# Five query projections moved into the last delta head, and the loads of the next six moved ahead of the attention block

## What is computed

```
p = x @ w_in                         # columns split among all heads
A: gated DeltaNet, 8 heads of 128    # q, k, v, z from p; causal conv; chunked delta rule
B: sparse attention, 16 query heads  # q = p[..., nq], K/V of three branches from p
h = sigmoid(gA) * o_A + sigmoid(gB) * o_B
x = LayerNorm(alpha * x + h @ w_out)
x = LayerNorm(alpha * x + MoE(x))    # 64 experts, top 6
```

## Time and profile before

| | |
|---|---|
| Time, median of 3 (lowest, highest) | 2173.21 us (2172.13, 2180.12) |
| The profiled execution's own time | 2190.67 us |
| Its span | 2188.9 us |
| PE busy | 1900.0 us, 87% |
| DVE, ACT, POOL busy | 798.4, 549.1, 336.3 us |
| Delta heads 0 to 7 | about 148 to 897 us of the span |
| Attention projections (L1391) | 904 to 1024 us of the span |

### The profile page before, as it was taken

One profiled execution on the slowest core, in us unless ns is written; L12 is line 12 of the kernel. 1 busy time (PEld: TensorE's weight loads), 2 busy tenths in 40 slices (PEclk: granted clock), 3 DMA queues, 4 the chain that ended last, 5 costly groups with the idle time before them and its releaser, 6 DMA issues. The chain is left out here.

```text
span 2188.9 us, 27560 instructions
## 1 busy us (share of the span) xinstructions
PE 1900.0 (87%) x10610; PEld 1295.2 (59%) x10610; DVE 798.4 (36%) x1903; ACT 549.1 (25%) x1266; POOL 336.3 (15%) x365
## 2 busy tenths in 40 slices
PE   7599989999898967799998897899998889888978
PEld 4277777777777756588886665546544333434423
DVE  0025444453444541101658874426322222222106
ACT  1121323313223131102656662402011111111110
POOL 0001011010100100100314544400111111111101
PEclk9799999998999975799998998999999999999998
DMA  3531102111021000740530014770699999999946
GB/s 107 161 92 30 50 22 59 52 30 51 22 59 32 1 22 0 169 103 11 161 111 6 1 59 154 250 264 22 282 384 420 417 417 403 407 411 403 402 160 260
DMA packets 160370, 353.95 MB, mean 162 GB/s; under 512 B 36488, under 2 KB 113968, under 8 KB 134320
## 3 DMA queue, kind: packets, MB, share of 16 engines
q1 hardware_dynamic: 140368, 291.88, 36.2%
q0 software_dynamic: 19872, 60.31, 7.7%
HBM read 333.09 MB, written 35.27 MB: 168 GB/s over the span
## 5 line engine op out<-in xcount | busy, mean ns | idle before, releaser
L720 PE MATMUL bank<-xT,arena 128*128 128x272 f32 x1280 | 326.6, 407 | 1.7 <-DMA arena<-in_w_in 1.1
L2488 PE MATMUL bank<-arena,kvt 128*64 128x512 f32 (+1 forms) x816 | 268.6, 630 | 45.0 <-issue 44.1
L720 PEld LDWEIGHTS bank<-xT,arena 128*128 128x128 f32 x1280 | 243.6, 197 | 48.7 <-DMA arena<-in_w_in 1.3
L2488 PEld LDWEIGHTS bank<-arena,kvt 128*64 128x64 f32 (+1 forms) x816 | 91.1, 152 | 185.3 <-issue 185.3
L1055 POOL TENSOR_TENSOR arena<-arena 128x512 f32<-128x512 f32 x48 | 52.4, 1092 | 645.4 <-DVE arena L1157 447.3
L1391 PE MATMUL bank<-xT,arena 128*128 128x272 f32 x512 | 119.6, 397 | 13.5 <-DMA arena<-in_w_in 13.5
L2567 PE MATMUL bank<-arena,kvt 128*64 128x512 f32 (+1 forms) x408 | 128.1, 598 | 2.4 <-issue 2.1
L2884 DVE SCALAR_TENSOR_TENSOR kvt<-kvt,arena,bank 128x256 f32<-128x256 f32 x37 | 17.8, 480 | 282.6 <-ACT kvt L2674 282.6
L1391 PEld LDWEIGHTS bank<-xT,arena 128*128 128x128 f32 x512 | 98.6, 193 | 34.2 <-DMA arena<-in_w_in 13.6
L2488 PE MATMUL bank<-xT,kvt 128*64 128x512 f32 (+1 forms) x208 | 104.5, 661 | 15.9 <-issue 15.9
L2340 POOL DMA_INDIRECT hT<-x_rows,rows_i x37 | 37.6, 1017 | 392.3 <-DVE rows_i L2815 392.3
(11 more groups left out here) (510 smaller groups left out, 3242.0 us busy)
## 6 DMA issues: line engine op xcount, KB each, us to landing
arena<-in_w_exp_gate SPq DMA_DIRECT2D x51, 1024.0 KB, 13.8
arena<-in_w_exp_up SPq DMA_DIRECT2D x51, 1024.0 KB, 27.3
arena<-in_w_exp_down SPq DMA_DIRECT2D x51, 1024.0 KB, 26.3
arena<-in_w_in SPq DMA_DIRECT2D x48, 512.0 KB, 4.1
kvt<-in_w_exp_down SPq DMA_DIRECT2D x13, 1024.0 KB
xT<-in_w_exp_gate SPq DMA_DIRECT2D x13, 1024.0 KB
xT<-in_w_exp_up SPq DMA_DIRECT2D x13, 1024.0 KB
arena<-y_rows SPq DMA_DIRECT2D x6, 1536.0 KB, 15.0
```

The lines of the kernel that those rows point to most:

```text
L720: last = mm(banks[2 * (i % 2) + half][:, 0:HALF], wh[blk % RING][:, k, :], xT[:, k, half * HALF:(half + 1) * HALF], start=(k == 0), stop=( ...
L2488: last = mm(banks[2 + 4 * (t % 2)][cols, :], xgT[:, k, cols], ewgu[i % EBUF][:, :, k], start=(k == 0), stop=(k == KD - 1))
```

## The change

It names five of the eight query blocks (`NQ_BEHIND` = 2, 3, 4, 5, 6) that are now computed behind the delta rule of head 7, with `part(8, j)`. `load_head(8)` loads them, `save_queries` copies them out into `qT` at once (the places of blocks 2 to 6 lie over the conv inputs `raw` of heads 6 and 7, so it waits until these have been read). The remaining three query blocks (0, 1, 7) and the eight merge blocks stay in the attention block, eleven in all (`ATT_BLOCKS`). The first six of the eleven are loaded in the delta block, in SP's stream of head 7, as their slots come free, and SP waits for these loads before it leaves the block. The other five are loaded in the attention block, behind `Wx` and `page_p`, which now come first.

```diff
+NQ_BEHIND, NQ_AHEAD = (2, 3, 4, 5, 6), (0, 1, 7)
+ATT_BLOCKS = len(NQ_AHEAD) + 8
...
+            def await_free(i):
+
+                done_h, m = divmod(i - RING, 5)
+                sp.wait_ge(pr_banked, 6 * done_h + (UNIT[m] if done_h < H else m) + 1)
...
+                    if h == H:
+                        load_query(sp, NQ_BEHIND[n], i, wh_in)
+                        continue
...
-                if h + 2 < H:
+                if h + 2 <= H:
                     load_head(h + 2)
+                if h == H - 1:
+                    for p in range(RING):
+                        await_free(FIRST_ATT + p)
+                        load_attention(sp, p, wh_in)
...
+            for i in range(FIRST_ATT, FIRST_ATT + RING):
+                sp.wait_ge(wh_in[i % RING], landed_by(i))
...
             def part(h, j):
 
-                if h == H:
-                    return
...
+            def save_queries(n):
+
+                i = 6 * H + n
+                if n == 0:
+                    sc.wait_ge(conv_done, H - 1)
+                    sc.wait_ge(cg_ready, H - 1)
+                if n == 2:
+                    sc.wait_ge(conv_done, H)
+                    sc.wait_ge(cg_ready, H)
+                sc.wait_ge(pr_banked, i + 1)
+                for half in range(2):
+                    last = actv(qT[:, NQ_BEHIND[n], half * HALF:(half + 1) * HALF], banks[2 * (i % 2) + half][:, 0:HALF], ACT.Copy)
+                last.then_inc(pr_saved, 1)
...
-            for n in range(16):
-                blk = n
-                pe.wait_ge(wh_in[blk % RING], 16 * sum(KVH if b < G else 1 for b in range(blk % RING, blk + 1, RING)))
+            for n in range(ATT_BLOCKS):
+                blk = FIRST_ATT + n
+                if n >= RING:
+                    pe.wait_ge(wh_in[blk % RING], 16)
```

The new loaders, called from SP's stream:

```diff
+        def load_query(sp, j, i, landed):
+
+            src = w_cols[:, :, COL_NQ:COL_NQ + D].rearrange("p k (g j d) -> j p k g d", g=KVH, j=G)[j]
+            for g in range(KVH):
+                sp.dma_start(wh[i % RING][:, :, g * HD:g * HD + HD], src[:, :, g]).then_inc(landed[i % RING], 16)
+
+        def load_merge(sp, m, i, landed):
+
+            c0 = COL_MG + D + m * P
+            sp.dma_start(wh[i % RING], w_cols[:, :, c0:c0 + P]).then_inc(landed[i % RING], 16)
+
+        def load_attention(sp, p, landed):
+
+            if p < len(NQ_AHEAD):
+                load_query(sp, NQ_AHEAD[p], FIRST_ATT + p, landed)
+            else:
+                load_merge(sp, p - len(NQ_AHEAD), FIRST_ATT + p, landed)
```

More of the change, by code:

```diff
@@ L497, in tok, with landed_by @@
             return (t * P, P if t < 4 else NS_TOK)
+        w_cols = io["w_in"][0].rearrange("(k p) n -> p k n", p=P)
+        def load_query(sp, j, i, landed):
[10 more added lines that the diff above has]
+                load_merge(sp, p - len(NQ_AHEAD), FIRST_ATT + p, landed)
+        FIRST_Q = 5 * H
+        FIRST_ATT = FIRST_Q + len(NQ_BEHIND)
+        def landed_by(i):
+            first_merge = FIRST_ATT + len(NQ_AHEAD)
+            return 16 * sum(2 if FIRST_Q <= b < first_merge else 1 for b in range(i % RING, i + 1, RING))
         def load_gate_up(sp, i, which):
@@ L630, in load_head @@
                     if i >= RING:
-                        done_h, m = divmod(i - RING, 5)
-                        sp.wait_ge(pr_banked, 6 * done_h + UNIT[m] + 1)
+                        await_free(i)
+                    if h == H:
+                        load_query(sp, NQ_BEHIND[n], i, wh_in)
+                        continue
                     sp.dma_start(wh[i % RING], w[:, :, c0 + h * P:c0 + h * P + P]).then_inc(wh_in[i % RING], 16)
+                if h == H:
+                    return
                 if h >= 2:
@@ L707, in part @@
             def part(h, j):
-                if h == H:
-                    return
                 n, quarter = divmod(j, 4)
                 half, k0 = quarter // 2, quarter % 2 * 4
-                i = 6 * h + UNIT[n]
+                i = 6 * h + (UNIT[n] if h < H else n)
                 blk = 5 * h + n
                 if quarter == 0:
-                    pe.wait_ge(wh_in[blk % RING], 16 * (blk // RING + 1))
+                    pe.wait_ge(wh_in[blk % RING], landed_by(blk))
                     if i >= 2:
@@ L909, in _ @@
             actv(convw[:, :], banks[5][:, 0:96], ACT.Copy).then_inc(cw_ready, 1)
+            def save_queries(n):
[10 more added lines that the diff above has]
+                last.then_inc(pr_saved, 1)
             def save(h, unit):
                 if h == H:
+                    if unit != 3:
+                        save_queries(UNIT.index(unit))
                     return
@@ L1310, in _ @@
         def _(sp):
-            w = io["w_in"][0].rearrange("(k p) n -> p k n", p=P)
             sp.dma_start(page_all[:, :], io["page_table"].rearrange("(o b) p -> o (b p)", o=1).to_broadcast([P, NB * NPG])).then_inc(ids_in, 16)
             sp.dma_start(quad_cmp, io["quad_cmp"]).then_inc(ids_in, 16)
-            for n in range(16):
[L1316 to L1333, removed]
+            w1 = io["nsa_cmp_w1"][0].rearrange("s (r j u d) e -> s r (u d) j e", r=2, j=8, u=2)
+            for s in range(2):
+                for r in range(2):
+                    sp.dma_start(Wx[:, s, :, r * HD:(r + 1) * HD], w1[s, r]).then_inc(w1_in, 16)
+            rows = cmp_rows.rearrange("(n a r) c -> a n (r c)", a=4, r=4)
+            for a in range(4):
+                sp.dma_start(page_p[32 * a:32 * a + 32], rows[a]).then_inc(rows_p_in, 16)
+            for p in range(RING, ATT_BLOCKS):
+                sp.wait_ge(prj_banked, p - RING + 1)
+                load_attention(sp, p, wh_in)
+            sp.wait_ge(prj_banked, ATT_BLOCKS)
             sp.dma_start(pos_rows[0:32], io["nsa_cmp_pos"][0].rearrange("s (m u) d -> (s m) (u d)", u=2)).then_inc(c2_in, 16)
@@ L1393, in _ @@
                 last.then_inc(prj_banked, 1)
-            pe.wait_ge(prj_saved, 16)
+            pe.wait_ge(prj_saved, ATT_BLOCKS)
             for br in range(2):
@@ L1674, in _ @@
             step = Steps(sc, act_step)
-            for n in range(16):
+            for n in range(ATT_BLOCKS):
                 sc.wait_ge(prj_banked, n + 1)
-                dst = qT[:, n] if n < 8 else mgB[:, n - 8]
+                dst = qT[:, NQ_AHEAD[n]] if n < len(NQ_AHEAD) else mgB[:, n - len(NQ_AHEAD)]
                 for half in range(2):
@@ L1681, in _ @@
                 last.then_inc(prj_saved, 1)
-            sc.wait_ge(prj_saved, 16)
+            sc.wait_ge(prj_saved, ATT_BLOCKS)
             actv(mgB, mgB, ACT.Tanh, scale=0.5)
```

## The result

The changed kernel took 2123.1 us (median of 4, 2113.9 to 2130.8), the kernel before 2175.0 us (median of 4) beside it: a ratio of 0.9727, 95% interval 0.9693 to 0.9762. In a second comparison on another occasion it was 2133.2 against 2183.9 us, 0.9765 (0.9728 to 0.9802). The ratios with an interval are estimates from all the runs and not quite the quotients of the medians (2123.1 by 2175.0 is 0.976). The forecast was 2120 us in a range of 2111 to 2129, a ratio of 0.976.

What follows compares the result with a forecast made beforehand. PE was taken as the bound, as work in filled heads and as slow work in empty head 7. Terms of -10.75, -5.97 and -36.67 us made -53.4, scaled to -53.0: 2173.2 to 2120.2 us, range 2111 to 2129.

Steps and rivals of the forecast that it cites:

- Term 1: Head 7: filling with 80 projection matmuls lifts the clock, so it takes 91.91 instead of 102.66 us, -10.75 us.
- PE goes from one step to the next with hardly a gap: Filled head 6: PE sets the pace, so less conv work on DVE and ACT in head 7 was priced at nothing.
- Rival 4: Head 7 runs shorter than any filled head, say 86 us, and the clock holds through the barrier: -61 us, 2112 us; 10%.
- Term 2: Attention block start: first six blocks' weights already in SBUF, so PE need not wait, -5.97 us.
- Term 3: Attention block: eleven projection blocks instead of sixteen, 5 x 7.33 = -36.67 us, with no late gather.
- Moved steps: SP's 19 more transfers in heads 6 and 7, reordered attention loads and ACT's moved copies: no extra cost, 0 us.
- Rival 1: Weights late in the filling or at SP's last wait, losing term 2 and some of term 1: -42 us, 2131 us; 7%.
- Sum: Whole kernel: the three terms together give -53.4 us on the profiled execution, -53.0 us at the median's scale.
- Rivals 2 and 3: Clock stays low in head 7 (2170 us, 2%), or attention's eleven blocks run at 1.2 GHz throughout (2200 us, 1%).

Runs made afterwards that it cites:

- the first pair: First traces of the kernel before and the changed kernel; 2175.0 against 2123.1 us in medians, ratio 0.9727.
- the second pair: The kernel before and the changed kernel each traced once more, with no new edit; changed kernel 2133.19 against 2183.92 us, ratio 0.9765.
- the loads alone: Kernel before with only the six attention loads moved ahead, head 7 empty, sixteen projections kept; 2183.4 against 2183.7 us, ratio 0.9999.

## Why the prediction was right, step by step

*Term 1* (-10.75 us, bounds -8.25 to -13.25): the traces of before and of the changed kernel give 102.66 and 101.11 against 91.23 and 92.67, -9.9 us between the means; the three traces with an empty head 7 and the six with 80 matmuls in it (84 in one of them) have means of 101.6 and 91.8 us, again -9.9. Mechanism and size hold; the run with idle filling shows that it is the clock. Two readings were rougher than the recorded text says. The level of 8.19 us is the longest of the unfilled head: from 830.76 on L809 starts 7.84, 6.88, 7.26 and 8.19 us apart, and in two of the levels its eight instructions took 1.13 us, as at full clock.

```profile
838.60 1.13 PE L809 MATMUL bank<-arena 128*128 128x128 f32 x8 [1.66 <-DVE arena L1171]
845.48 1.13 PE L809 MATMUL bank<-arena 128*128 128x128 f32 x8 [1.67 <-DVE arena L1171]
```

So the empty head switches between the two levels of the clock, as its mean of 0.63 says. And one slice over the filled heads stands at eight tenths and not at nine; by windows the seven filled heads have 0.93 to 0.98.

Where I gave the reason why head 7 would not run shorter than the others, I was wrong about what bounds a filled level: I read "PE goes from one step to the next with hardly a gap" as PE being the bound, while the runs with 20 and 40 matmuls show a level of the same length with PE waiting 1.20 and 0.74 us for DVE in it. It made no difference to the sum, as the filling was five whole blocks. Rival 4 (a head of 86 us, from less work on DVE and ACT) did not come with the full filling; heads of 88.0 and 88.6 us were seen with less filling, one trace each; the shortest fully filled head in any trace took 88.8 us.

*Term 2* (-5.97 us): 6.1 us with and without the loads ahead at a filled head, 6.2 us at an empty one. The first 4 us stayed below full clock, as taken (0.59; 0.50 before).

*Term 3* (-36.67 us): from the opening to the K transposes 126.4 became 83.3 us, -43.1 for terms 2 and 3 together, 42.6 forecast. No gather and no weight was waited for: the only transfer that PE waits for in the stretch is the small one it waited for before (L1452, 1.31 us).

*Moved steps* (0): confirmed by where the loads stand in SP's timeline and by the run with the loads at the end. Rival 1 (late weights) would have been real for another place of the same loads: 10.9 us of the 53.

*Sum*: 53.4 us forecast on the profiled execution, 53.7 us measured at the K transposes (1024.38 against 970.72). So close a match is in part luck: counted from the end of head 6 the first pair gives 54.5 us, the two pairs together 53.2. The span itself shrank by 59.9 us; of the 6.2 us more behind the K transposes only 1.9 us came back in the second pair, some 1.5 of them in the row L1440, so most of it was chance. The medians shrank by 51.9 and 50.7 us. It is luck too that the time itself came out: on the second occasion the two kernels were 9 and 10 us slower, and 2133.2 us is outside the range of 2111 to 2129, while the ratio held. Rivals 2 and 3 (a clock that stays low in the head, or throughout the attention block) are out by the windows.

## What to carry to other kernels

In this kernel PE was busy for 67% of a head of dependent steps and still made it long, at a granted clock of 0.63; with more work in it the head was 9.9 us shorter. So compare the granted clock of a stretch with that of a neighbour that does the same steps plus other work, and price the filling from that neighbour as a whole. The filling paid twice here, once for itself (36.7 us out of the attention block) and once for the chain it stands in (9.9 us). Where no useful work is at hand, idle matmuls may do: 80 of them gave the second part, and in one trace each 20 and 40 did as well. Loads for the stage behind a barrier are best issued where their slot comes free: behind the last store the same loads cost 10.9 us.

## What the hardware showed that I had not expected

How little filling lifts the clock: 20 matmuls of 272 columns (9.2 us of work in a head of 88.6 us) took the granted clock from 0.64 to 0.83, 40 to 0.89 and 80 to 0.95, and PE's whole busy time with 20 (66.58 us) was no more than that of the empty head (67.19 us).

How much filled heads differ by themselves: heads 1 to 6, with the same instructions on PE, took 88.8 to 94.1 us in the eleven traces. Head 6 alone took 91.8 to 91.9 us in five of them, 93.3 us in three (the second of before, the first of the changed kernel, the loads alone), 89.5 to 89.6 us in two and 88.8 us in the one with 20 idle matmuls in head 7. This adds up: head 6 ended at 774.6 us in one trace and at 792.3 us in another, 18 us apart, where the total of one kernel scattered by 17 and 29 us. What decides it was not tried.
